# A macaron block on one core: the normed activations 64 bytes short of the weights' address remainder, their 512-column products made as two of 256

## The chip, the cores and the metric

The kernel runs on one core of one Trainium2 chip. The time is the device time of one execution in microseconds (us), as the median of several runs. Before the change it is 1037.92 us, the median of 3 runs from 1037.42 to 1038.10.

## The reference

The input x is one sequence of 512 tokens with 1024 features in float32. One layer is computed, and a final norm:

```python
x = x + 0.5 * swiglu(rms_norm(x, ffn1_norm), ffn1_w_gate, ffn1_w_up, ffn1_w_down)    # 1024 -> 2816 -> 1024
h = rms_norm(x, mix_norm)
z, xbc, dt_raw, u = split(h @ w_in)                     # 1024, 1536, 16 and 1024 columns
y_ssd = ssd_group(z, xbc, dt_raw, ...)                  # conv, scan over chunks, gate, grouped norm
y_pool = multiscale_pool_group(u, pool_w, pool_scale)   # trailing means, a map for each group
x = x + concat([y_ssd, y_pool]) @ w_out
x = x + 0.5 * swiglu(rms_norm(x, ffn2_norm), ffn2_w_gate, ffn2_w_up, ffn2_w_down)
return rms_norm(x, final_norm)
# swiglu(h, wg, wu, wd) = (silu(h @ wg) * (h @ wu)) @ wd
```

## The kernel before

Activations lie feature by feature: a tile is 128 features (partitions) by 512 tokens (columns), and x has DK = 8 such tiles in `xT`. All large products are made with float32 operands that are split into a high part (fp32r) and what is left of it: `whi` and `wlo` for weights, `xghi` and `xglo` for the normed input ("normed" is x times the gain; the division by the root mean square comes later, through `rstd`). A product of two such pairs takes three matmuls: whi by hi, whi by lo, wlo by hi. Each matmul has its own weight load of 128 x 128, also where the weights are the same as in the matmul before.

The work is a sequence of units. A unit has one slot of a ring of RING = 4 in `whi` and `wlo`, holding 8 weight blocks of 128 x 128. ScalarE rounds a fetched weight into `whi` (lines 644, 653, 657), VectorE subtracts to get `wlo` (lines 967, 972), and TensorE waits for both through the semaphores `w_hi` and `w_lo`. A unit of 512 columns has 24 matmuls of 512 columns. Each engine's order is written out by hand.

Each of the two feed-forward stages (FFN1, FFN2) first computes some gate and up units directly: `direct`, by way of `products` (lines 1525 to 1540), 512 columns from `xghi` and `xglo`. FFN1 has 8 such units, of which the first four are computed in pieces by `part` at the start of the kernel (lines 1675 to 1692, matmuls on 1684, 1687, 1690), and FFN2 has 4. The rest of gate and up is made in "quads": two tiles of gate and up together, as a 2 x 2 block product (blocks of features by token halves) with seven products where eight would be the plain way (Strassen's scheme, Winograd's form). FFN1 has 9 quads and FFN2 has 10. A quad is seven units A11, SUM1, SUM2, A12, SUM3, SUM4, A22 by `product` (matmuls on lines 1601 to 1603), each of 24 matmuls of 256 columns. A11, A12 and SUM4 stream halves of `xghi` and `xglo`; SUM1, SUM2, SUM3 and A22 stream `thi` and `tlo`, combinations of the normed input that are made once in each stage. After the quads of a group come eight down units (lines 1619 to 1621), 512 columns from `acthi` and `actlo`; there are three groups in a stage. VectorE gathers the results of the quads (line 1062), forms the sums of weights (lines 1033 to 1055) and the activations, and GpSimd scales gates by `rstd` (line 547).

Between the two stages lies the mixer. `dt_unit` (lines 1785 to 1797) makes a short product of 512 columns from `xghi` and `xglo`. Then 12 + 16 units go through `project` (the convolved channels, z and u), with small products for the scan between them, then the pooled maps, then 8 units of the output projection of the pooled half, and 8 units of that of the other half, from `mixhi` and `mixlo`. In the first two of these groups and in the 8 pooled units the moving operand is `xghi` and `xglo` by 512 columns (lines 1537 to 1539).

Buffers are placed by hand in part. `sb(...)` puts tensors one behind the other: `whi`, `wlo`, `xT`, `xghi`, `xglo`, `rstd`, `sq`, `sumsq`, `ones`, and so on, down to small ones. The tensors placed by `at(...)` have given offsets from `base`. The remainder of an address by 256 bytes is named in constants: WEIGHT_LANE = 128 and HALF_LANE = 192, with LANES = 256.

```python
base += (WEIGHT_LANE - base) % LANES
acthi = at("acthi", 16 * KB, [P, UB * S], F32R)
thi = at("thi", 64 * KB + HALF_LANE, [P, 4, KH, HALF], F32R)
tlo = at("tlo", 80 * KB + HALF_LANE, [P, 4, KH, HALF], F32R)
```

So `whi`, `wlo`, `xghi`, `xglo`, `acthi`, `actlo`, `mixhi`, `mixlo` start at remainder 128. `thi` and `tlo` start at (128 + 192) mod 256 = 64, and `post` and `gbuf` too. All blocks within these tensors are multiples of 512 bytes long, so the remainder is the same for each block of them.

Of the kernel before, what the change touches and what calls it, by code (L numbers as in the profile page):

```python
# [23 lines left out]
P = 128  # L24
S = 512
D = 1024
DK = D // P
# [4 lines left out]
HEADS = 16  # L32
# [3 lines left out]
LOW = 32  # L36
# [4 lines left out]
HALF = S // 2  # L41
# [8 lines left out]
UB = 8  # L50
LANES = 256
WEIGHT_LANE = 128
HALF_LANE = 192
# [68 lines left out]
U_OUTP = U_POOL + 2  # L122
U_OUTS = U_OUTP + DK
M_FFN2 = M_MIX + U_OUTS + DK
# [71 lines left out]
U_ORDER = (6, 7, 4, 5, 2, 3, 0, 1)  # L196
# [3 lines left out]
def cols(tile):  # L200

    return slice(tile * S, (tile + 1) * S) if isinstance(tile, int) else bass.ds(tile * S, S)
# [10 lines left out]
def build(nc, t, out):  # L213
    with ExitStack() as ctx:
        def sb(name, shape, dt=F32):
            return ctx.enter_context(nc.sbuf_tensor(name, shape, dt))
# [5 lines left out]
        whi = sb("w_hi_part", [P, RING, UB, P], F32R)  # L222
        wlo = sb("w_lo_part", [P, RING, UB, P], F32R)
        xT = sb("xT", [P, DK * S])
        xghi = sb("xghi", [P, DK * S], F32R)
        xglo = sb("xglo", [P, DK * S], F32R)
        rstd = sb("rstd", [P, S])
# [6 lines left out]
        eps = sb("eps", [P, 1])  # L234
        inv_count = sb("inv_count", [P, PAD])
        dt_bias = sb("dt_bias", [2 * LOW, 1])
        fold = sb("fold", [2 * LOW, HEADS])
        a_exp = sb("a_exp", [P, HEADS])
        skip_row = sb("skip_row", [P, HEADS])
        skip_col = sb("skip_col", [P, DK])  # L240
        tok_rms = sb("tok_rms", [P, 2, NC])
        neg_gain = sb("neg_gain", [P, 2, DK])
# [70 lines left out]
        PB = [ctx.enter_context(nc.psum_tensor(f"bank{i}", [P, S], F32)) for i in range(8)]  # L313
# [66 lines left out]
        def slot(m):  # L380
            return m % RING
# [25 lines left out]
        def half(h):  # L407
            return slice(h * HALF, (h + 1) * HALF)
# [1112 lines left out]

        @blk.tensor
        def _(pe):
            def products(bank, m, i, blocks, hi, lo, k0, first=True, last=True, ready=None,
                         order=None, midway=None):

                pe.wait_ge(w_hi, i * RING + (m + 1))
                pe.wait_ge(w_lo, i * RING + (m + 1))
                s = slot(m)
                for n, k in enumerate(order or range(blocks)):  # L1530
                    if midway and n == blocks // 2:
                        midway()
                    if ready:
                        pe.wait_ge(ready[0], ready[1] + n + 1)
                    h, l = hi[:, cols(k0 + k)], lo[:, cols(k0 + k)]
                    w, wl = whi[:, s, k, :], wlo[:, s, k, :]
                    pe.matmul(bank, w, h, start=first and n == 0, stop=False)  # L1537
                    pe.matmul(bank, w, l, start=False, stop=False)  # L1538
                    mm = pe.matmul(bank, wl, h, start=False, stop=last and n == blocks - 1)  # L1539
                mm.then_inc(unit_done, 1)  # L1540
# [6 lines left out]
            def direct(f, it, n):  # L1547

                tile, bank = it.tile, it.raw % 4
                if f == 0:  # L1550
                    pe.wait_ge((g_scaled, act_ready)[it.part], tile - 1)
                products(PB[bank][:, :], n, 0, UB, xghi, xglo, 0, ready=(xg_lo, 2 * DK) if n == M_FFN2 else None)

            def moving(f, part, k):

# [121 lines left out]
            def part(m, *ks):  # L1677

                bank = PB[m][:, :]
                h = ks[0] // (UB // 2)  # L1680
                pe.wait_ge((first_hi, w_hi)[h], m + 1)
                for k in ks:
                    pe.wait_ge(xg_hi, k + 1)
                    pe.matmul(bank, whi[:, m, k, :], xghi[:, cols(k)], start=k == 0, stop=False)
                for k in ks:
                    pe.wait_ge(xg_lo, k + 1)
                    pe.matmul(bank, whi[:, m, k, :], xglo[:, cols(k)], start=False, stop=False)
                pe.wait_ge((first_lo, w_lo)[h], m + 1)
                for k in ks:
                    mm = pe.matmul(bank, wlo[:, m, k, :], xghi[:, cols(k)], start=False, stop=k == DK - 1)  # L1690
                if ks[-1] == DK - 1:
                    mm.then_inc(unit_done, 1)

# [30 lines left out]
            M = M_MIX  # L1724
# [6 lines left out]
            def project(m, ready=None, midway=None):  # L1731
                if m >= 2:
                    pe.wait_ge(proj_read, m - 1)
                products(PB[m % 2][:, :], M + m, 0, UB, xghi, xglo, 0, ready=ready, midway=midway)

            def chunks_to_tokens(bank, src, width=P, off=0, rows=P):
                for c in range(NC):
# [136 lines left out]
            for d in range(DK):  # L1874
                if d >= 2:
                    pe.wait_ge(proj_read, U_POOL + d - 1)
                products(PB[(U_OUTP + d) % 2][:, :], M + U_OUTP + d, 0, UB, xghi, xglo, 0,
                         ready=(pool_lo, 0) if d == 0 else None, order=U_ORDER if d == 0 else None)
                if d == 3:
                    for g in range(GROUPS):  # L1880
                        pe.wait_ge(ysum_own, 2 + 4 * (g + 1))
                        pe.matmul(scratch(SC[f"stat{g}"])[:, :], ones[:, :], cbuf[:, g, :],
                                  start=True, stop=True).then_inc(scr_ready, 1)
# [72 lines left out]
```

## Time and profile before

| | |
|---|---|
| median of 3 runs | 1037.92 us |
| the profiled execution | 1038.42 us |
| its span (first to last instruction) | 1036.6 us |
| TensorE matmul busy | 999.3 us (96%), 6118 matmuls |
| TensorE weight loads busy | 878.2 us (85%), 6118 loads |
| VectorE busy | 781.8 us (75%) |
| ScalarE, GpSimd busy | 462.3 us (45%), 212.0 us (20%) |
| mean granted TensorE clock | 0.983 of full |

Durations of matmuls overlap: a matmul of 512 columns is shown with some 0.39 us and one of 256 with 0.28 us, but the next one starts before it ends. So the pace of TensorE is read from the starts of matmuls or of whole units, and not from the mean durations. All times in the views are from the start of the span.

### The profile page before, as it was taken

To read this page: it belongs to the slowest core of one execution; us is meant where nothing else is said; L and a number is where in the kernel's file an instruction comes from. 1 tells how busy PE (TensorE), PEld (TensorE's weight loads), DVE (VectorE), ACT (ScalarE), POOL (GpSimd) and SP (SyncE) were. 2 spreads that over 40 slices of the span, in tenths; PEclk is the share of its full clock that TensorE was granted. 3 is DMA by queue.
4 is the path that set the end of the run, shared out by engine and by line. 5 is a ranking of instruction groups with operands and counts; after the bars stand their busy time and mean duration, and the time that the engine had idled before them with its cause. 6 is when DMAs were issued, how large, how long until landed. Compare 5 with 4: busy or idle time off the path is not lost. (4 is left out here: it accounts for less than half of the span.)

```text
span 1036.6 us, 15358 instructions
## 1 busy us (share of the span) xinstructions
PE 999.3 (96%) x6118; PEld 878.2 (85%) x6118; DVE 781.8 (75%) x983; ACT 462.3 (45%) x603; POOL 212.0 (20%) x179
## 2 busy tenths in 40 slices
PE   9979999999999989999999999879999999999996
PEld 7879889998999658878787888759988999889975
DVE  5788568985697778787699796677966798567864
ACT  6455225552354446653234653344632455325532
POOL 1003002320031242321063452101110113001321
PEclk9989999999999989999999999979999999999998
DMA  8405313442232242322322233422252225412402
GB/s 270 138 24 158 104 41 110 136 143 82 61 103 62 64 125 84 94 65 78 82 82 68 75 89 95 122 82 82 83 162 82 82 82 153 134 41 85 119 21 82
DMA packets 188655, 99.63 MB, mean 96 GB/s; under 512 B 3524, under 2 KB 187944, under 8 KB 188584
## 3 DMA queue, kind: packets, MB, share of 16 engines
q1 hardware_dynamic: 187912, 97.60, 32.2%
q8 instruction: 49, 0.80, 0.3%
q10 hardware_dynamic: 672, 1.05, 0.3%
q14 instruction: 22, 0.18, 0.1%
HBM read 96.54 MB, written 2.10 MB: 95 GB/s over the span
## 5 line engine op out<-in xcount | busy, mean ns | idle before, releaser
L547 POOL TENSOR_TENSOR post<-post,rstd 128x256 f32<-128x256 f32 x57 | 93.3, 1637 | 536.5 <-DVE post L1062 536.5
L1601 PE MATMUL bank<-thi,w_hi_part 128*128 128x256 f32 x608 | 169.5, 279 | 5.8 <-DVE tlo L1023 3.6
L1602 PE MATMUL bank<-tlo,w_hi_part 128*128 128x256 f32 x608 | 168.9, 278 | 0.0
L1603 PE MATMUL bank<-thi,w_lo_part 128*128 128x256 f32 x608 | 168.7, 277 | 0.0
L1537 PE MATMUL bank<-xghi,w_hi_part 128*128 128x512 f32 x352 | 143.5, 408 | 10.4 <-DVE xglo L977 10.4
L972 DVE TENSOR_TENSOR w_lo_part<-w_raw,w_hi_part 128x1024 fp32r<-128x1024 f32 (+1 forms) x102 | 124.8, 1224 | 22.0 <-ACT w_hi_part L644 12.3
L1619 PE MATMUL bank<-acthi,w_hi_part 128*128 128x512 f32 x346 | 136.2, 394 | 4.4 <-DVE upd L1103 2.4
L1538 PE MATMUL bank<-xglo,w_hi_part 128*128 128x512 f32 x352 | 138.5, 393 | 0.0
L1539 PE MATMUL bank<-xghi,w_lo_part 128*128 128x512 f32 x352 | 138.4, 393 | 0.0
L1621 PE MATMUL bank<-acthi,w_lo_part 128*128 128x512 f32 x346 | 134.8, 390 | 0.0
L1620 PE MATMUL bank<-actlo,w_hi_part 128*128 128x512 f32 x346 | 134.7, 389 | 0.0
L1603 PE MATMUL bank<-xghi,w_lo_part 128*128 128x256 f32 x456 | 128.8, 282 | 0.0
L1601 PE MATMUL bank<-xghi,w_hi_part 128*128 128x256 f32 x456 | 128.7, 282 | 0.0
L1602 PE MATMUL bank<-xglo,w_hi_part 128*128 128x256 f32 x456 | 128.4, 282 | 0.0
L1601 PEld LDWEIGHTS bank<-thi,w_hi_part 128*128 128x128 f32 x608 | 115.0, 189 | 6.4 <-DVE tlo L1023 3.8
L1602 PEld LDWEIGHTS bank<-tlo,w_hi_part 128*128 128x128 f32 x608 | 115.1, 189 | 0.0
L1603 PEld LDWEIGHTS bank<-thi,w_lo_part 128*128 128x128 f32 x608 | 114.9, 189 | 0.0
L653 ACT ACTIVATE w_hi_part<-w_raw 128x1024 fp32r<-128x1024 f32 x76 | 80.3, 1056 | 73.9 <-PE bank L1603 38.9
L967 DVE TENSOR_TENSOR w_lo_part<-w_raw,w_hi_part 128x1024 fp32r<-128x1024 f32 x76 | 106.0, 1401 | 0.0
L657 ACT ACTIVATE w_hi_part<-w_raw 128x1024 fp32r<-128x1024 f32 (+1 forms) x56 | 55.9, 998 | 112.3 <-PE bank L1621 74.0
L1103 DVE SCALAR_TENSOR_TENSOR upd<-bank,rstd 128x512 f32<-128x512 f32 (+1 forms) x49 | 33.2, 677 | 91.6 <-PE bank L1621 91.1
L653 ACT ACTIVATE w_hi_part<-wsum 128x1024 fp32r<-128x1024 f32 x57 | 60.3, 1058 | 76.6 <-PE bank L1603 41.6
(260 smaller groups left out, 1958.1 us busy)
## 6 DMA issues: line engine op xcount, KB each, us to landing
w_raw<-in_ffn_w_gate SPq DMA_DIRECT2D x42, 512.0 KB, 3.7
w_raw<-in_ffn_w_up SPq DMA_DIRECT2D x42, 512.0 KB, 4.6
w_raw<-in_ffn_w_down SPq DMA_DIRECT2D x32, 512.0 KB, 4.4
w_raw<-in_w_in SPq DMA_DIRECT2D x29, 512.0 KB, 3.6
w_raw<-in_w_out SPq DMA_DIRECT2D x16, 512.0 KB, 3.9
w_raw<-in_ffn_w_down SPq DMA_DIRECT2D x16, 384.0 KB, 4.1
out<-xtok SPq DMA_DIRECT2D x4, 512.0 KB, 3.1
xload<-in_x SPq DMA_DIRECT2D x3, 512.0 KB, 6.7
```

What stands on the lines that cost most here:

```text
L653: act.activation(split(whi, n), weight(q, it.part), ACT.Copy).then_inc(w_hi, 1)
L967: dve.tensor_tensor(split(wlo, n), weight(it.quad, it.part), split(whi, n).bitcast(F32), ALU.subtract).then_inc(w_lo, 1)
L972: dve.tensor_tensor(wlo[:, slot(n), 0:blocks], raw[:, src, 0:blocks], whi[:, slot(n), 0:blocks].bitcast(F32), ALU.subtract).then_inc(w_lo, 1)
L1537: pe.matmul(bank, w, h, start=first and n == 0, stop=False)
L1538: pe.matmul(bank, w, l, start=False, stop=False)
L1539: mm = pe.matmul(bank, wl, h, start=False, stop=last and n == blocks - 1)
L1601: pe.matmul(out, w, hi, start=opens and e == 0 and k == 0, stop=False, skip_group_check=True)
L1602: pe.matmul(out, w, lo, start=False, stop=False, skip_group_check=True)
L1603: mm = pe.matmul(out, wl, hi, start=False, stop=end, skip_group_check=True)
L1619: pe.matmul(bank, whi[:, s, k, :], h, start=first and k == ks[0], stop=False)
L1620: pe.matmul(bank, whi[:, s, k, :], l, start=False, stop=False)
L1621: mm = pe.matmul(bank, wlo[:, s, k, :], h, start=False, stop=last and k == ks[-1])
```

## The change

The small tensors `fold`, `a_exp` and `skip_row` (64 bytes in each partition, 192 in all) move from behind `dt_bias` to a place ahead of `xghi`. By this `xghi`, `xglo`, `rstd`, `sq`, `sumsq`, `ones`, `ident`, `causal`, `par`, `eps`, `inv_count` and `dt_bias` lie 192 bytes further, at remainder 64 for those that were at 128. `skip_col` and all that follows stays where it was. Every product whose moving operand is `xghi` or `xglo` by 512 columns (in `part`, `direct`, `project` and the pooled half of the output projection) is made as two matmuls of 256 columns, into the two halves of the same bank: the first half of the columns and then the second, with the same weights, before the next of the three products. The short product in `dt_unit` keeps its 512 columns. The products of the quads, of down and from `mixhi` keep their form.

```diff
--- before.py
+++ after.py
@@ -222,6 +222,10 @@
         whi = sb("w_hi_part", [P, RING, UB, P], F32R)
         wlo = sb("w_lo_part", [P, RING, UB, P], F32R)
         xT = sb("xT", [P, DK * S])
+        fold = sb("fold", [2 * LOW, HEADS])
+        a_exp = sb("a_exp", [P, HEADS])
+        skip_row = sb("skip_row", [P, HEADS])
+        assert nc.sbuf_base % LANES == (WEIGHT_LANE + HALF_LANE) % LANES
         xghi = sb("xghi", [P, DK * S], F32R)
         xglo = sb("xglo", [P, DK * S], F32R)
         rstd = sb("rstd", [P, S])
@@ -234,9 +238,6 @@
         eps = sb("eps", [P, 1])
         inv_count = sb("inv_count", [P, PAD])
         dt_bias = sb("dt_bias", [2 * LOW, 1])
-        fold = sb("fold", [2 * LOW, HEADS])
-        a_exp = sb("a_exp", [P, HEADS])
-        skip_row = sb("skip_row", [P, HEADS])
         skip_col = sb("skip_col", [P, DK])
         tok_rms = sb("tok_rms", [P, 2, NC])
         neg_gain = sb("neg_gain", [P, 2, DK])
@@ -1521,6 +1522,27 @@
 
         @blk.tensor
         def _(pe):
+            def both_halves(bank, w, x, k, start=False, stop=False):
+                for h in range(2):
+                    mm = pe.matmul(bank[:, half(h)], w, x[:, k * S + h * HALF:k * S + (h + 1) * HALF],
+                                   start=start and h == 0, stop=stop, skip_group_check=True)
+                return mm
+
+            def from_norm(bank, m, ready=None, order=None, midway=None):
+
+                pe.wait_ge(w_hi, m + 1)
+                pe.wait_ge(w_lo, m + 1)
+                s = slot(m)
+                for n, k in enumerate(order or range(UB)):
+                    if midway and n == UB // 2:
+                        midway()
+                    if ready:
+                        pe.wait_ge(ready[0], ready[1] + n + 1)
+                    both_halves(bank, whi[:, s, k, :], xghi, k, start=n == 0)
+                    both_halves(bank, whi[:, s, k, :], xglo, k)
+                    mm = both_halves(bank, wlo[:, s, k, :], xghi, k, stop=n == UB - 1)
+                mm.then_inc(unit_done, 1)
+
             def products(bank, m, i, blocks, hi, lo, k0, first=True, last=True, ready=None,
                          order=None, midway=None):
 
@@ -1549,7 +1571,7 @@
                 tile, bank = it.tile, it.raw % 4
                 if f == 0:
                     pe.wait_ge((g_scaled, act_ready)[it.part], tile - 1)
-                products(PB[bank][:, :], n, 0, UB, xghi, xglo, 0, ready=(xg_lo, 2 * DK) if n == M_FFN2 else None)
+                from_norm(PB[bank][:, :], n, ready=(xg_lo, 2 * DK) if n == M_FFN2 else None)
 
             def moving(f, part, k):
 
@@ -1681,13 +1703,13 @@
                 pe.wait_ge((first_hi, w_hi)[h], m + 1)
                 for k in ks:
                     pe.wait_ge(xg_hi, k + 1)
-                    pe.matmul(bank, whi[:, m, k, :], xghi[:, cols(k)], start=k == 0, stop=False)
+                    both_halves(bank, whi[:, m, k, :], xghi, k, start=k == 0)
                 for k in ks:
                     pe.wait_ge(xg_lo, k + 1)
-                    pe.matmul(bank, whi[:, m, k, :], xglo[:, cols(k)], start=False, stop=False)
+                    both_halves(bank, whi[:, m, k, :], xglo, k)
                 pe.wait_ge((first_lo, w_lo)[h], m + 1)
                 for k in ks:
-                    mm = pe.matmul(bank, wlo[:, m, k, :], xghi[:, cols(k)], start=False, stop=k == DK - 1)
+                    mm = both_halves(bank, wlo[:, m, k, :], xghi, k, stop=k == DK - 1)
                 if ks[-1] == DK - 1:
                     mm.then_inc(unit_done, 1)
 
@@ -1731,7 +1753,7 @@
             def project(m, ready=None, midway=None):
                 if m >= 2:
                     pe.wait_ge(proj_read, m - 1)
-                products(PB[m % 2][:, :], M + m, 0, UB, xghi, xglo, 0, ready=ready, midway=midway)
+                from_norm(PB[m % 2][:, :], M + m, ready=ready, midway=midway)
 
             def chunks_to_tokens(bank, src, width=P, off=0, rows=P):
                 for c in range(NC):
@@ -1874,8 +1896,8 @@
             for d in range(DK):
                 if d >= 2:
                     pe.wait_ge(proj_read, U_POOL + d - 1)
-                products(PB[(U_OUTP + d) % 2][:, :], M + U_OUTP + d, 0, UB, xghi, xglo, 0,
-                         ready=(pool_lo, 0) if d == 0 else None, order=U_ORDER if d == 0 else None)
+                from_norm(PB[(U_OUTP + d) % 2][:, :], M + U_OUTP + d,
+                          ready=(pool_lo, 0) if d == 0 else None, order=U_ORDER if d == 0 else None)
                 if d == 3:
                     for g in range(GROUPS):
                         pe.wait_ge(ysum_own, 2 + 4 * (g + 1))
```

## Rows read from the trace of the kernel before

**Rows 1.** The page's first part: busy time of each engine.

```profile
PE 999.3 (96%) x6118; PEld 878.2 (85%) x6118; DVE 781.8 (75%) x983; ACT 462.3 (45%) x603; POOL 212.0 (20%) x179
```

**Rows 2.** TensorE groups by line and shape: busy us, mean ns, idle before, releasers.

```profile
L1601 PE MATMUL bank<-thi,w_hi_part 128*128 128x256 f32 x608 | 169.5, 279 | 5.8 <-DVE tlo L1023 3.6 <-DVE w_lo_part L967 1.9 <-ACT post L701 0.3
...
L1537 PE MATMUL bank<-xghi,w_hi_part 128*128 128x512 f32 x352 | 143.5, 408 | 10.4 <-DVE xglo L977 10.4
...
L1619 PE MATMUL bank<-acthi,w_hi_part 128*128 128x512 f32 x346 | 136.2, 394 | 4.4 <-DVE upd L1103 2.4 <-DVE actlo L1000 1.6
...
L1601 PE MATMUL bank<-xghi,w_hi_part 128*128 128x256 f32 x456 | 128.7, 282 | 0.0
```

**Rows 3.** TensorE's timeline: first matmuls of A11, SUM1, SUM2, A12.

```profile
187.16 0.28 PE L1601 MATMUL bank<-xghi,w_hi_part 128*128 128x256 f32 x1
...
190.02 0.29 PE L1601 MATMUL bank<-thi,w_hi_part 128*128 128x256 f32 x1
...
192.76 0.28 PE L1601 MATMUL bank<-thi,w_hi_part 128*128 128x256 f32 x1
...
195.48 0.28 PE L1601 MATMUL bank<-xghi,w_hi_part 128*128 128x256 f32 x1
```

**Rows 4.** Timeline of TensorE: first matmuls of two direct units, 24 matmuls apart.

```profile
40.40 0.39 PE L1537 MATMUL bank<-xghi,w_hi_part 128*128 128x512 f32 x1
...
45.84 0.39 PE L1537 MATMUL bank<-xghi,w_hi_part 128*128 128x512 f32 x1
```

**Rows 5.** TensorE's timeline: halves of the last down unit, matmuls 1 and 9.

```profile
1019.68 0.28 PE L1925 MATMUL bank<-acthi,w_hi_part 128*128 128x256 f32 x1
...
1020.63 0.28 PE L1927 MATMUL bank<-acthi,w_lo_part 128*128 128x256 f32 x1
```

**Rows 6.** One quad's window: us, PE, PEld, DVE, ACT, POOL, clock, DMA, GB/s.

```profile
187.16:206.68 19.52, 19.52 (x171) 19.52 (x169) 18.83 (x21) 11.03 (x14) 4.98 (x4) 1.00 0.39 115
```

**Rows 7.** Timeline of VectorE in that quad.

```profile
196.30 1.21 DVE L967 TENSOR_TENSOR w_lo_part<-wsum,w_hi_part 128x1024 fp32r<-128x1024 f32 x1
...
198.54 0.69 DVE L1062 TENSOR_TENSOR post<-post,bank 128x512 f32<-128x512 f32 x1 [0.69 <-PE bank L1603]
...
200.28 1.76 DVE L967 TENSOR_TENSOR w_lo_part<-w_raw,w_hi_part 128x1024 fp32r<-128x1024 f32 x1
```

**Rows 8.** Timeline of TensorE in the first quad: two stalls.

```profile
61.65 0.35 PE L1601 MATMUL bank<-thi,w_hi_part 128*128 128x256 f32 x1 [1.90 <-DVE w_lo_part L967]
...
66.50 0.58 PE L1601 MATMUL bank<-thi,w_hi_part 128*128 128x256 f32 x1 [3.56 <-DVE tlo L1023]
```

**Rows 9.** The chain of waits ahead of FFN2's first down unit.

```profile
760.33 1.15 DVE actlo L1000
761.62 0.47 PE bank L1619
```

**Rows 10.** TensorE's timeline: restarts behind small products, 512 and 256 columns.

```profile
390.75 0.50 PE L1537 MATMUL bank<-xghi,w_hi_part 128*128 128x512 f32 x1
391.09 0.39 PE L1538 MATMUL bank<-xglo,w_hi_part 128*128 128x512 f32 x1
...
1022.36 0.36 PE L1925 MATMUL bank<-acthi,w_hi_part 128*128 128x256 f32 x1
1022.56 0.28 PE L1926 MATMUL bank<-actlo,w_hi_part 128*128 128x256 f32 x1
```

**Rows 11.** Timeline of TensorE: the short product's last stall.

```profile
374.69 0.63 PE L1794 MATMUL bank<-xglo,w_hi_part 128*32 128x512 f32 x1 [4.51 <-DVE xglo L977]
```

**Rows 12.** Groups by line and shape: ScalarE, sources and targets at different remainders.

```profile
L653 ACT ACTIVATE w_hi_part<-w_raw 128x1024 fp32r<-128x1024 f32 x76 | 80.3, 1056 | 73.9 <-PE bank L1603 38.9 <-PE bank L1621 35.0
...
L693 ACT ACTIVATE thi<-t 128x1024 fp32r<-128x1024 f32 x8 | 8.5, 1060 | 19.2 <-DVE t L1011 19.2
```

**Rows 13.** Windows at the lower clock (columns as in rows 6).

```profile
674.00:687.70 13.70, 6.17 (x13) 4.18 (x14) 8.40 (x11) 7.31 (x9) 1.26 (x1) 0.50 0.38 112
373.60:380.50 6.90, 5.81 (x12) 3.79 (x13) 5.59 (x4) 3.53 (x4) 6.61 (x6) 0.51 0.52 149
```

## The prediction

> **What bounds the kernel now.** I began with the busy times on the page: TensorE matmuls 999.3 of 1036.6 us, no other engine over 76% [rows 1]. The groups by line say whether the rest can matter: with all the idle time ahead of them, the product lines wait 5.8 us for thi, 10.4 us for the 512-column products from xghi, 4.4 us in down, and nothing for the 256-column products from xghi [rows 2]. So the end is set by the pace at which TensorE streams matmuls, stage after stage. That pace is not the mean duration (matmuls overlap in the rows, and by their means two of 256 columns would look dearer, 2 x 279 ns, than one of 512 with 408 ns [rows 2]), so I read starts on the timeline.
>
> In a quad all units have 24 matmuls of 256 columns, the same shape and the same number of weight loads. From the start of A11 to that of SUM1 there are 190.02 - 187.16 = 2.86 us, SUM1 takes 2.74 us, SUM2 2.72 us [rows 3]. The pattern repeats to 10 ns in all steady quads: a unit that streams xghi and xglo takes 2.86 us (119.2 ns a matmul), one that streams thi and tlo takes 2.74 us directly behind an xghi unit and 2.72 us otherwise (113.3 ns). What differs in the code is the address remainder of the moving operand: 128 as the weights, or 64. The last down unit checks this: it streams acthi, remainder 128, by 256 columns, from a quite different place in memory, and its eight intervals take 0.95 us, 118.8 ns each [rows 5]. So 119 ns goes with the weights' own remainder, 113.3 with the other.
>
> A unit of 24 matmuls of 512 columns at remainder 128 takes 45.84 - 40.40 = 5.44 us [rows 4], 226.7 ns a matmul. That is twice 113.3.
>
> **The change part by part.**
>
> *256-column units from xghi (A11, A12, SUM4).* They come to remainder 64 with no other edit. There are 57 of them, three in each of 19 quads. I price them as SUM2: 2.86 - 2.72 = 0.14 us less. SUM1, SUM3 and A22 no longer follow a slower unit: 2.74 - 2.72 = 0.02 us less each. A steady quad goes from 19.52 us [rows 6] to 7 x 2.72 = 19.04 us, 0.48 us less. The cost of an xghi unit at the new place is not in the trace; below it is bounded by a loss of nothing seen (2.86 us stays), above by 2.72, and I take 2.72, the row with the same shape, engine and remainder.
>
> Quads with the full gain: 18 x 0.48 = 8.64 us. The first quad of FFN1 is different: SUM1 waits for w_lo until 61.65 and then for tlo until 66.50 [rows 8], VectorE's work, so A11's gain there goes into the stall. A12 to A22 keep 2 x 0.14 + 2 x 0.02 = 0.32 us. At the end of the six groups the chain runs from the gather after SUM4 through VectorE to actlo, which ends last, 761.62 [rows 9]; what A22 saves there is waited for instead: 6 x 0.02 = 0.12 us back. Sum: 8.64 + 0.32 - 0.12 = 8.84 us.
>
> *Does VectorE keep up?* In a middle quad it is busy 18.83 of 19.52 us, idle 0.69 [rows 6], and that idle time is a wait for TensorE's bank [rows 7]. Two quads, the middle ones of FFN1's second group and of FFN2's second group, are that tight; the others are idle 1.2 us or more. A gain of 0.48 us leaves 0.21 us idle, so VectorE stays just behind TensorE and not ahead of it. The cover is thin: one w_lo subtraction in that quad took 1.76 us [rows 7]. I take no loss; the other end is below, as a rival.
>
> *512-column products as two of 256.* 48 units: the 4 of `part`, 4 direct in FFN1, 4 direct in FFN2, 28 of `project`, 8 of the pooled output projection, so 48 x 24 = 1152 matmuls become 2304, with 1152 more weight loads. In steady flow 2 x 113.3 = 226.6 ns against 226.7 ns: nothing. More weight loads cost nothing at that pace, since the thi units keep one load per 256 columns at 113.3 ns. Alternating between the halves of a bank, where the quads write one half for 12 matmuls, is not shown; the 512-column matmul writes both in turn, and I take it as free. The ends for this edit: at 119.2 ns a half, 2 x 119.2 - 226.7 = 11.7 ns more for each of 1152, 13.5 us slower; below, as far under the thi rows as the xghi rows are over them, 107.4 ns a half, 13.7 us faster (an estimate of mine for the end only); the thi rows have shape and remainder in common with what is made, and I keep them.
>
> *Restarts.* Behind small products the first interval of a unit is 0.34 us for 512 columns against 0.227 in flow, 0.11 more; for 256 columns 0.20 against 0.12, 0.08 more [rows 10]. About 20 units of the mixer start so: 20 x 0.03 = 0.6 us less. I take 0.5, with ends at 0 and 1.2 (the following intervals are some ns slow as well by 512 columns).
>
> *The short product* keeps 512 columns at remainder 64, which no row shows. It waits for xglo in any case, 4.51 us at its last block [rows 11]; two matmuls follow, so even twice their time is under 0.5 us. I take 0.
>
> *Engines that read or write the moved tensors.* ScalarE's copy of 1024 columns takes 1056 ns from w_raw into whi and 1060 ns from t32 into thi, at other remainders on both sides [rows 12]. So a new remainder costs ScalarE nothing here; I take the same for VectorE and GpSimd. No wait, DMA or queue order changes.
>
> *The sum.* 8.84 + 0.5 = 9.3 us less. From the profiled 1038.42 us (span 1036.6) that is 1029.1 us. That execution lies 0.5 us above the median shown, so the forecast is 1037.9 - 9.3 = **1028.6 us**.
>
> *Two rules weighed.* The equality 226.7 = 2 x 113.3 is from rows 3 and 4. The Trainium skill, "TensorE: Matmul & The Clock Gate", section "Back-to-back issue gap", gives a warm gap of the columns by 2.4 GHz plus 2.5 ns for each matmul; by that, 1152 more matmuls would cost 2.9 us, and the sum would be 6.4 us less instead of 9.3. The trace disagrees with its figures (215.8 and 109.2 ns against 226.7 and 113.3). That page also has a sustained roofline of 131 ns for 512 columns with their loads, which the trace contradicts (226.7 ns).
>
> **The rivals.**
>
> *A: halves cost as the other halves at 119 ns (slower).* If the remainder is not what parts the two kinds of unit, but something that thi has and xghi has not, xghi stays at 119.2 ns after the move. Then the quads gain nothing and the split costs 1152 x 11.7 ns = 13.5 us, less 0.5 for restarts: 1051 us. The price falls in `part`, the direct units, `project` and the pooled projection, and decides from the first product on; the whole change turns slower as soon as a matmul of 256 columns from xghi takes over 115.8 ns, 2.5 above 113.3 (9.3 us over the 57 x 24 in the quads and the 2304 halves). For it: no row shows xghi at 64. Against it: acthi, which is neither in xghi's place nor in thi's, goes with its remainder [rows 5]. The Trainium skill, "SBUF — State Buffer", section "Who interferes with whom", gives TensorE two independent read ports, for moving operand and weight load, and says that it never waits on anyone; by that rule a remainder could change nothing and this rival would hold. Rows 3 speak against the rule.
>
> *B: VectorE becomes the bound in the quads.* If collisions with GpSimd stretch its work (1.76 us against 1.21 us for the same shape [rows 7]), TensorE would wait for w_lo, and half of the quads' gain would turn into idle time ahead of line 1601: 8.84 / 2 + 0.5 = 4.9 us less, 1033 us. For it: 0.21 us of cover. Against: only two quads are so tight.
>
> *C: the clock's low stretches move.* TensorE ran at the lower level, 1.2 GHz, from 674.0 to 687.7 us with 6.17 us of matmuls and from 373.6 to 380.5 with 5.81 us [rows 13], each behind a stall. Work at half speed loses half of its time, 3.1 and 2.9 us. Stages now begin 4 and 9 us earlier, and the switch back may come earlier or later against the work: one stretch longer by half gives 1.5 us more, 1030.2 us, and shorter ones up to 3 us less, 1025.6 us. Small shifts of this kind belong to the forecast's own range.
>
> **How the numbers follow.** Forecast 0.74, with its own range of 1027 to 1030.5 us; A 0.08; B 0.08; C, off by over 1.5 us, 0.10. The range reaches from 1025.5 (C below, restarts at their end) to 1034 (B); A stays outside. A measurement of this kernel tells about 0.2%, 2.1 us, from no change. Faster by more: forecast, C and most of B, 0.89. Within: 0.03. Slower: 0.08, A.
>
> **What would show it.** The starts of A11 and SUM1 2.72 us apart and a steady quad of 19.04 us; direct and `project` units still 5.44 us, now with 48 matmuls; some 7270 matmuls in all, and weight loads close to 100% busy in the mixer; VectorE idle some 0.2 us in the tight quads with no wait for w_lo ahead of TensorE there; the stall before 66.50 us unchanged at its end. Units of 2.86 us in the quads and 5.72 us in `project` would make it wrong (A), and waits of line 1601 for w_lo in each quad would show B.

## The result, and the profile after

The change makes the kernel slower: median 1040.47 us (1039.08 to 1045.20, 14 runs) against 1037.91 us (1036.39 to 1038.72, 14 runs). The ratio is 1.0034, 95% interval 1.0022 to 1.0046, some 3.5 us (the medians alone are 2.6 us apart). The forecast was 1028.6 us, the range 1025.5 to 1034. The profiled execution took 1044.33 us with a span of 1042.6 us, 3.9 us above the median of its kernel; why is among the findings. Times are more spread than before, 6.1 us from lowest to highest against 2.3 us.

The page's first part and four groups of TensorE by line and shape answer to [rows 1, 2]. Line 1527 is the helper `both_halves`.

```profile
PE 1006.6 (97%) x7270; PEld 934.7 (90%) x7270; DVE 781.8 (75%) x983; ACT 461.4 (44%) x603; POOL 212.0 (20%) x179
```

```profile
L1623 PE MATMUL bank<-thi,w_hi_part 128*128 128x256 f32 x608 | 171.8, 283 | 5.9 <-DVE tlo L1024 3.6 <-DVE w_lo_part L968 2.1 <-ACT post L702 0.3
...
L1527 PE MATMUL bank<-xghi,w_hi_part 128*128 128x256 f32 x768 | 154.8, 287 | 10.7 <-DVE xglo L978 10.3 <-ACT xghi L662 0.3
...
L1641 PE MATMUL bank<-acthi,w_hi_part 128*128 128x512 f32 x346 | 136.3, 394 | 3.9 <-DVE upd L1104 2.3 <-DVE actlo L1001 1.4
...
L1623 PE MATMUL bank<-xghi,w_hi_part 128*128 128x256 f32 x456 | 127.9, 280 | 0.0
```

There are 7270 matmuls, as computed, and the waits are the old ones to 0.5 us. But the mean of the thi products rose from 279 to 283 ns, though neither `thi` nor its products were touched. That line is the first sign: the loss is in TensorE's pace and not in a wait. The timeline of TensorE, first matmuls of units, shows two paces. First an xghi unit and the thi unit behind it, in the first group of FFN1, then A11, SUM1, SUM2 and A12 of quad 4 (compare [rows 3]), then two units of the pooled output projection, then two more (compare [rows 4]):

```profile
79.77 0.28 PE L1623 MATMUL bank<-xghi,w_hi_part 128*128 128x256 f32 x1
...
82.49 0.28 PE L1623 MATMUL bank<-thi,w_hi_part 128*128 128x256 f32 x1
...
85.21 0.28 PE L1623 MATMUL bank<-xghi,w_hi_part 128*128 128x256 f32 x1
...
188.01 0.28 PE L1623 MATMUL bank<-xghi,w_hi_part 128*128 128x256 f32 x1
...
190.84 0.28 PE L1623 MATMUL bank<-thi,w_hi_part 128*128 128x256 f32 x1
...
193.67 0.28 PE L1623 MATMUL bank<-thi,w_hi_part 128*128 128x256 f32 x1
...
196.50 0.28 PE L1623 MATMUL bank<-xghi,w_hi_part 128*128 128x256 f32 x1
...
580.30 0.28 PE L1527 MATMUL bank<-xghi,w_hi_part 128*128 128x256 f32 x1
...
585.95 0.28 PE L1527 MATMUL bank<-xghi,w_hi_part 128*128 128x256 f32 x1
...
610.09 0.28 PE L1527 MATMUL bank<-xghi,w_hi_part 128*128 128x256 f32 x1
...
615.53 0.28 PE L1527 MATMUL bank<-xghi,w_hi_part 128*128 128x256 f32 x1
```

Near 80 us a unit takes 2.72 us, 113.3 ns a matmul, as forecast. Near 190 us each unit takes 2.83 us, 117.8 ns, whether it streams xghi or thi. The same is seen for 48 matmuls: 5.65 us at 580 and 5.44 us at 610, from the same buffers by the same line. In the quads, a pace holds from the start of an unbroken stretch of 256-column matmuls to its end; in the mixer some units take up to five intervals to settle. Group 1 of FFN1 ran at the fast one; groups 2 and 3 of FFN1 and all of FFN2's quads at the slow one, 17 of 19 quads. In the mixer 16 of 36 units ran at the slow one. A slow steady quad takes 19.79 us, where it was 19.52 us [rows 6] and 19.04 us was forecast.

Where the 6.0 us between the two profiled spans came from, by the starts of the same units on the two timelines:

| place | before | after | added since the row above |
|---|---|---|---|
| first unit after `part` | 34.95 | 35.81 | +0.85 |
| quad 2 (FFN1's second group) | 148.11 | 148.44 | -0.52 |
| short product | 365.94 | 367.96 | +1.69 |
| quad 9 (FFN2's first) | 702.47 | 706.11 | +1.62 |
| last group of down in FFN2 | 986.46 | 992.45 | +2.35 |

The two rows that hold nothing but slow quads and down units, +1.69 and +2.35, are 4.0 of the 6.0 us.

### The profile page after: what moved, and what is told of

Same layout as the page of the kernel before. It is cut to its first block and busy times, and to the rows that moved or that the text cites. A ratio compares the mean times of both kernels' runs of the same rounds, so it can differ in the third digit from the quotient of the medians.

```text
span 1042.6 us, 17662 instructions
## 1 busy us (share of the span) xinstructions
PE 1006.6 (97%) x7270; PEld 934.7 (90%) x7270; DVE 781.8 (75%) x983; ACT 461.4 (44%) x603; POOL 212.0 (20%) x179
## 5 line engine op out<-in xcount | busy, mean ns | idle before, releaser
L1623 PE MATMUL bank<-thi,w_hi_part 128*128 128x256 f32 x608 | 171.8, 283 | 5.9 <-DVE tlo L1024 3.6
L1624 PE MATMUL bank<-tlo,w_hi_part 128*128 128x256 f32 x608 | 171.3, 282 | 0.0
L1625 PE MATMUL bank<-thi,w_lo_part 128*128 128x256 f32 x608 | 171.2, 282 | 0.0
L1527 PE MATMUL bank<-xghi,w_hi_part 128*128 128x256 f32 x768 | 154.8, 287 | 10.7 <-DVE xglo L978 10.3
L1527 PE MATMUL bank<-xghi,w_lo_part 128*128 128x256 f32 x768 | 148.8, 280 | 0.7 <-DVE w_lo_part L1182 0.6
L1527 PE MATMUL bank<-xglo,w_hi_part 128*128 128x256 f32 x768 | 149.4, 280 | 0.1
L1527 PEld LDWEIGHTS bank<-xghi,w_hi_part 128*128 128x128 f32 x768 | 117.5, 190 | 17.6 <-DVE xglo L978 10.7
L1623 PE MATMUL bank<-xghi,w_hi_part 128*128 128x256 f32 x456 | 127.9, 280 | 0.0
L1624 PE MATMUL bank<-xglo,w_hi_part 128*128 128x256 f32 x456 | 127.9, 280 | 0.0
L1625 PE MATMUL bank<-xghi,w_lo_part 128*128 128x256 f32 x456 | 127.9, 280 | 0.0
L1625 PEld LDWEIGHTS bank<-thi,w_lo_part 128*128 128x128 f32 x608 | 117.3, 193 | 0.0
L1527 PEld LDWEIGHTS bank<-xghi,w_lo_part 128*128 128x128 f32 x768 | 116.0, 189 | 1.1 <-DVE w_lo_part L1182 1.1
L1527 PEld LDWEIGHTS bank<-xglo,w_hi_part 128*128 128x128 f32 x768 | 116.6, 190 | 0.3 <-DVE xglo L978 0.3
```

The costliest lines, as they stand in the source:

```text
L1527: mm = pe.matmul(bank[:, half(h)], w, x[:, k * S + h * HALF:k * S + (h + 1) * HALF], start=start and h == 0, stop=stop, skip_group_check=True)
L1623: pe.matmul(out, w, hi, start=opens and e == 0 and k == 0, stop=False, skip_group_check=True)
L1624: pe.matmul(out, w, lo, start=False, stop=False, skip_group_check=True)
L1625: mm = pe.matmul(out, wl, hi, start=False, stop=end, skip_group_check=True)
```

## The experiments

Ratios are against runs of the kernel before on the same chip. Theory P says: a stream of 256-column matmuls, each with its weight load, has more than one steady pace, and which one it holds is set when it is entered.

**Split alone.** `fold`, `a_exp` and `skip_row` go back behind `dt_bias`.

```diff
-        fold = sb("fold", [2 * LOW, HEADS])
-        a_exp = sb("a_exp", [P, HEADS])
-        skip_row = sb("skip_row", [P, HEADS])
...
         xghi = sb("xghi", [P, DK * S], F32R)
...
         dt_bias = sb("dt_bias", [2 * LOW, 1])
+        fold = sb("fold", [2 * LOW, HEADS])
+        a_exp = sb("a_exp", [P, HEADS])
+        skip_row = sb("skip_row", [P, HEADS])
```

> The 512-column products from xghi are made as two of 256, and nothing is moved (xghi stays at remainder 128). Theory P (two paces: a stream of 256-column matmuls with its weight loads runs at 113.3 or at 117.8 ns a matmul at remainder 64, whichever it falls into when it is entered, and at 119 to 120 ns at remainder 128): each of the 48 split units takes 48 x 119.8 = 5.75 us instead of 5.44 us, some 13 us slower in all, 1050 to 1051 us, and the quads stay at 19.52 us with thi at 113.3 ns. Rival S (the split itself is free, and what slows the changed kernel is the place of the moved tensors): about 1037 us. Rival H (the doubled number of instructions slows TensorE's queue): some 4 us slower, without a change of pace in steady flow.

Measured: 1048.70 us, ratio 1.0105 (1.0088 to 1.0122), 10.8 us slower. Its timeline, two direct units, 5.76 us apart:

```profile
42.09 0.28 PE L1526 MATMUL bank<-xghi,w_hi_part 128*128 128x256 f32 x1
...
47.85 0.28 PE L1526 MATMUL bank<-xghi,w_hi_part 128*128 128x256 f32 x1
```

That is 120 ns a matmul at remainder 128, in all of the split units, and the quads stayed at 19.52 us. So the remainder does matter, as the prediction had it. The steady price is 0.32 us a unit, 15 us for all 48, of which the median shows 10.8. Part of the rest is seen on the timeline: the stall of FFN1's first quad took up 1.4 us (that quad starts 2.66 us late and takes 1.37 us less), restarts are shorter by halves, and FFN2's first direct unit took 6.71 us where it was 7.69, behind 3.60 us of matmuls at the lower clock where [rows 13] have 6.17.

**Move alone.** All products keep their form, the small tensors stay ahead of `xghi`.

Against the kernel before, the move is all of the edit:

```diff
         xT = sb("xT", [P, DK * S])
+        fold = sb("fold", [2 * LOW, HEADS])
+        a_exp = sb("a_exp", [P, HEADS])
+        skip_row = sb("skip_row", [P, HEADS])
...
         xghi = sb("xghi", [P, DK * S], F32R)
```

> xghi, xglo and their neighbours are moved to remainder 64, and all products keep their 512 columns. Theory P: the quads are one stream at remainder 64 that is entered behind 512-column down units without a gap, so 117.8 ns a matmul and 19.79 us a quad in five of the six groups, 4 to 5 us slower in the quads; the direct and projecting units show what 512 columns cost at remainder 64, which nothing has shown yet (226.7 ns if the remainder doesn't matter there): 1041 us or more. Rival H (the split is what costs): the quads run at 113.3 ns, 19.04 us each, and the time is near 1029 us. Rival S: as theory P in sign, but thi and xghi units of a quad at different paces.

Measured: 1043.81 us, ratio 1.0061 (1.0045 to 1.0078). The timeline: two direct units of 512 columns, then A11 of quads 4, 5, 9 and 10.

```profile
40.94 0.40 PE L1538 MATMUL bank<-xghi,w_hi_part 128*128 128x512 f32 x1
...
46.54 0.40 PE L1538 MATMUL bank<-xghi,w_hi_part 128*128 128x512 f32 x1
...
188.41 0.28 PE L1602 MATMUL bank<-xghi,w_hi_part 128*128 128x256 f32 x1
...
208.19 0.28 PE L1602 MATMUL bank<-xghi,w_hi_part 128*128 128x256 f32 x1
...
707.17 0.28 PE L1602 MATMUL bank<-xghi,w_hi_part 128*128 128x256 f32 x1
...
726.22 0.28 PE L1602 MATMUL bank<-xghi,w_hi_part 128*128 128x256 f32 x1
```

The 512-column products cost 5.60 us a unit, 233.3 ns each, at remainder 64, against 5.44 us [rows 4]; those from `mixhi`, which did not move, stayed at 226.7 ns in the same run. So the split was needed for them: even slow halves (5.65 us) lose hardly more, and fast halves (5.44 us) nothing. Quads are slow (19.79 us) in five groups with no split anywhere, so it isn't the split that slows them. Only FFN2's first group is fast (19.04 us).

**The changed kernel again.**

> The changed kernel once more, for a second profile. Theory P: the stretches right behind 512-column units (the quads of the second and third groups of FFN1 and of the groups in FFN2) run at 117.8 ns again, and those behind a wait or small products (the units of the mixer, the first group of FFN1) run at 113.3 or 117.8 in another pattern than in the first profile, which makes the spread of its times (1039 to 1045 us). Rival S or H: the same pace in the same stretches, and the spread is not in TensorE's pace.

Measured: 1040.60 us (1040.13 to 1044.03), ratio 1.0030 (1.0018 to 1.0043). Its timeline has quad 9 fast, 19.04 us, where the first profile had 19.79 us:

```profile
704.79 0.28 PE L1623 MATMUL bank<-xghi,w_hi_part 128*128 128x256 f32 x1
...
723.83 0.28 PE L1623 MATMUL bank<-xghi,w_hi_part 128*128 128x256 f32 x1
```

The same program thus had another pace in the same stretch (FFN2's direct units with quads 9 to 11): that stretch starts behind the stall for xglo. The groups behind down units were slow again. FFN1's first group, also entered from a stall, was slow this time and fast in the first profile. The mixer's units had the same pace in both. The first profile is 4.3 us longer. The stretch in FFN2 makes 3.2 us of it, 2.7 by the pace and 0.5 by more matmuls at the lower clock in its first unit; FFN1's first group makes 0.9 us the other way. The first unit behind the short product (7.72 against 6.83 us, from matmuls at the lower clock) adds 0.9, and the last matmuls of the kernel, 213 against 112 ns each, 0.8. So the spread of the times has two parts, as far as two profiles show: the pace in stretches that start behind a stall, and where the lower clock ends or begins.

**Extra matmuls of several sizes.** One matmul with a discarded result, ahead of A11 in 15 quads.

```diff
+KICK = {3: 8, 4: 16, 5: 32, 6: 64, 7: 96, 8: 128, 10: 192, 11: 224, 12: 48, 13: 24, 14: 80, 15: 112, 16: 160, 17: 2, 18: 64}
...
+                if part == A11 and q in KICK:
+                    pe.matmul(PB[7][:, 0:KICK[q]], whi[:, slot(n), 0, :], xghi[:, 0:KICK[q]], start=True, stop=True)
```

> The changed kernel with one extra small matmul ahead of A11 in 15 of the 19 quads, into a bank that nobody reads: 8, 16, 32, 64, 96, 128 columns in quads 3 to 8, and 192, 224, 48, 24, 80, 112, 160, 2, 64 in quads 10 to 18. Theory P: the pace changes at some of these places, between 113.3 and 117.8 ns, and holds until the next one or the end of the stretch; quads at 113.3 take 19.04 us. Rival S or H: the pace stays as it was and the extra matmul costs its own time of some 0.1 us.

Measured: one run, 1037.02 us. The timeline at quads 3, 4 and 5, behind 8, 16 and 32 extra columns, then quad 6 and quad 18, each with its 64 extra columns and the starts of A11 and SUM1:

```profile
167.43 0.36 PE L1626 MATMUL bank<-xghi,w_hi_part 128*128 128x256 f32 x1
...
187.30 0.17 PE L1617 MATMUL bank<-xghi,w_hi_part 128*128 128x16 f32 x1
187.33 0.36 PE L1626 MATMUL bank<-xghi,w_hi_part 128*128 128x256 f32 x1
...
206.47 0.18 PE L1617 MATMUL bank<-xghi,w_hi_part 128*128 128x32 f32 x1
206.50 0.36 PE L1626 MATMUL bank<-xghi,w_hi_part 128*128 128x256 f32 x1
...
270.46 0.19 PE L1617 MATMUL bank<-xghi,w_hi_part 128*128 128x64 f32 x1
270.49 0.36 PE L1626 MATMUL bank<-xghi,w_hi_part 128*128 128x256 f32 x1
...
273.32 0.28 PE L1626 MATMUL bank<-thi,w_hi_part 128*128 128x256 f32 x1
...
965.69 0.19 PE L1617 MATMUL bank<-xghi,w_hi_part 128*128 128x64 f32 x1
965.72 0.36 PE L1626 MATMUL bank<-xghi,w_hi_part 128*128 128x256 f32 x1
...
968.63 0.28 PE L1626 MATMUL bank<-thi,w_hi_part 128*128 128x256 f32 x1
```

Quad 3 stays slow (19.87 us with its extra matmul), quad 4 turns fast (19.14), quad 5 slow again. Over all 15: behind 16, 64 (quad 6), 128, 192, 224, 24, 112 and 2 columns the quad ran fast, behind 8, 32, 96, 48, 80, 160 and 64 (quad 18) slow. The same 64 columns thus led to 2.83 us for A11 and a fast quad at one place and to 2.91 us and a slow quad at the other, so the size alone doesn't decide. What differs is the stream before: quad 6 follows down units, quad 18 a fast quad. Of the 12 extra matmuls put between two quads nine turned the pace over (16, 128, 24, 112 and 2 columns from slow to fast; 32, 96, 80 and 64 from fast to slow), and three left it (8 slow; 192 and 224 fast). Behind down units 64 led to fast, 48 and 160 to slow. An otherwise idle matmul of some 0.1 us can switch the next stretch in either direction. Theory P holds; the rivals that blame the split or the place don't.

**64 extra columns at 14 entries, and 48 as a control.** Into the unit's own bank, whose first product clears it.

```diff
+KICK = 64
...
+                if part == A11 and (not QUADS[q].chained) and q:
+                    pe.matmul(bank[:, 0:KICK], whi[:, slot(n), 0, :], xghi[:, 0:KICK], start=True, stop=True)
...
-                project(U_Z + h)
+                project(U_Z + h, kick=KICK if h % 2 else 0)
...
+                          kick=KICK if d == 0 else 0)
```

> The changed kernel with one extra matmul of 64 columns (from xghi, with the first weights of the unit, into the unit's own bank before its first product) in front of 14 streams that are entered behind 512 columns: A11 of the first quad of five groups (quads 2, 6, 9, 12, 16), the eight odd z and u units, and the first unit of the pooled output projection. Theory P (two paces, chosen at the entry): with this size each stretch of quads falls into 113.3 ns a matmul, as quads 6 and 18 did behind 64 columns, so 17 quads take 19.04 us and not 19.79 us, 12.8 us less than with all of them slow; the extra matmuls cost 0.12 us each, 1.7 us; 12 units of the mixer at 5.44 us give back up to 2.5 us. Together 1029 to 1033 us, faster than before. Rival (the pace is chosen anew at random at each entry, or the 64 columns were luck): some of the five stretches stay at 117.8 ns, and the time is between 1036 and 1042 us with a wide spread.

> As the kernel with 64 extra columns, but with 48. Theory P with the phase of the stream as what decides: 48 columns put quad 12 at 117.8 ns, so the stretches of quads stay slow behind this size, and the time is 1040 to 1046 us. Rival (any extra matmul breaks the pattern): as with 64 columns, 1029 to 1033 us.

Measured with 64: 1033.95 us (1032.90 to 1035.23), ratio 0.9964 (0.9951 to 0.9978). With 48: one run, 1046.58 us. Both lie up to 1 us above the ranges expected. The first timeline is of 64 columns, A11 of quads 3 and 4, then of 9 and 10; the second of 48, quads 3 and 4.

```profile
167.33 0.28 PE L1628 MATMUL bank<-xghi,w_hi_part 128*128 128x256 f32 x1
...
186.37 0.28 PE L1628 MATMUL bank<-xghi,w_hi_part 128*128 128x256 f32 x1
...
700.81 0.36 PE L1628 MATMUL bank<-xghi,w_hi_part 128*128 128x256 f32 x1
...
720.68 0.28 PE L1628 MATMUL bank<-xghi,w_hi_part 128*128 128x256 f32 x1
```

```profile
168.79 0.28 PE L1628 MATMUL bank<-xghi,w_hi_part 128*128 128x256 f32 x1
...
188.58 0.28 PE L1628 MATMUL bank<-xghi,w_hi_part 128*128 128x256 f32 x1
```

With 64 columns all four groups entered behind 512-column down units are fast (19.04 us a quad), with 48 all four are slow (19.79 us). The expectation that all five kicked stretches of quads would be fast missed one: quad 9 follows FFN2's direct units, which ran fast here, and the extra matmul threw it into the slow pace (19.87 us). That expectation also took it that quads 6 and 18 had both run fast behind 64 columns; quad 18, entered like quad 9 from a fast stream, had not. In the mixer the eight extra matmuls gained nothing either: seven of the eight units behind them ran at the slow pace. The one at the pooled output projection made its first four units fast and left the last four, fast in the changed kernel, slow.

**Other remainders.** HALF_LANE = 128 and 64, with as many small tensors moved as it takes.

Moving operands are then at remainder 0 and 192, the weights at 128 as before.

```diff
-HALF_LANE = 192
+HALF_LANE = 128
```

```diff
-HALF_LANE = 192
+HALF_LANE = 64
```

> The changed kernel with HALF_LANE = 128 instead of 192: xghi, xglo, thi and tlo (and the tensors behind them) at remainder 0 while the weights stay at 128. It asks whether the second pace is tied to the distance of 64 bytes short. Theory P leaves open which pace another distance has; if it is a matter of when loads and streams of the same 256 bytes meet, the steady pace is another one here (between 113.3 and 120 ns) and the same in all stretches, or there are two again in other stretches. Rival (only 'not the same remainder' matters): the same two paces in the same stretches as at 64, about 1040 us.

> The changed kernel with HALF_LANE = 64: moving operands at remainder 192, 64 bytes past the weights' 128. As for remainder 0: another set of paces if the order in which the two reads come to the same place matters (64 past is not the mirror of 64 short), or the same two paces, about 1040 us, if only the difference matters.

Measured: 1058.22 us, ratio 1.0192 (1.0177 to 1.0208), at remainder 0; 1048.40 us, ratio 1.0100 (1.0085 to 1.0116), at 192. A11 of quads 4 and 5, first at remainder 0, 20.16 us, 120.0 ns a matmul, then at 192, 19.79 us:

```profile
190.70 0.28 PE L1623 MATMUL bank<-xghi,w_hi_part 128*128 128x256 f32 x1
...
210.86 0.28 PE L1623 MATMUL bank<-xghi,w_hi_part 128*128 128x256 f32 x1
```

```profile
189.27 0.28 PE L1623 MATMUL bank<-xghi,w_hi_part 128*128 128x256 f32 x1
...
209.06 0.28 PE L1623 MATMUL bank<-xghi,w_hi_part 128*128 128x256 f32 x1
```

Remainder 0 has two paces as well: 120.0 ns in the quads behind down units and in FFN2, 118.7 ns in FFN1's first group, where a unit takes 2.85 us, and in most units of the mixer. At 192 all quads are slow, FFN1's first group and FFN2's too, and 32 of the mixer's 36 units. It has the narrowest spread (1048.28 to 1048.54). Of the four remainders tried (128 is the split alone), only 64 has the fast pace in whole groups, and it is the best. The weights stayed at remainder 128 in all of them, so it isn't shown whether the moving operand's own remainder counts or its distance from that of the weights.

**64 extra columns at five entries.** Against the kernel with 14 of them, without quad 9 and without the mixer's eight units.

```diff
-                if part == A11 and (not QUADS[q].chained) and q:
+                if part == A11 and q in (2, 6, 12, 16):
...
-                project(U_Z + h, kick=KICK if h % 2 else 0)
+                project(U_Z + h)
```

> The changed kernel with the extra matmul of 64 columns in five places only: A11 of quads 2, 6, 12 and 16, whose stretches begin behind the 512-column down units and ran at 113.3 ns with it, and the first unit of the pooled output projection. Left out are quad 9, which the extra matmul threw from the fast into the slow pace, and the eight units of the mixer, which it did not make faster. Theory P: 9 x 0.12 = 1.1 us less than with 14 extra matmuls, and the first group of FFN2 is left to its entry: 1030.5 to 1033.5 us, at least 4 us faster than before, with a spread of some 2 us by that group. Rival (the stretches fall into a pace at random in each program): some of the four stretches run at 117.8 ns and the time is 1035 us or more.

Measured: 1031.52 us (1030.14 to 1033.70), ratio 0.9937 (0.9924 to 0.9951). It is faster than before by 6.4 us and than the changed kernel by some 9. All 19 quads run at the fast pace here. The gain comes from the four entries of quads: at the pooled output projection three units turned fast and five slow, where the changed kernel had four of each. Its window of quad 4:

```profile
186.72:205.75 19.03, 19.03 (x170) 19.03 (x169) 18.80 (x21) 11.20 (x14) 4.95 (x4) 1.00 0.38 113
```

**The kernel before, with extra matmuls ahead of SUM1.** Nothing moved, nothing split.

```diff
+KICK = {1: 8, 2: 16, 3: 32, 4: 64, 5: 96, 6: 128, 7: 48, 8: 24, 9: 80, 10: 112, 11: 160, 12: 2, 13: 192, 14: 224, 15: 40, 16: 56, 17: 72, 18: 88}
...
+                if part == SUM1 and q in KICK:
+                    pe.matmul(bank[:, 0:KICK[q]], whi[:, slot(n), 0, :], thi[:, 0, 0, 0:KICK[q]], start=True, stop=True)
```

> The kernel before, nothing moved and nothing split, with one extra matmul (from thi) of another number of columns in front of SUM1 in quads 1 to 18, where the moving operand changes from xghi at remainder 128 to thi at remainder 64. Theory P (113.3 ns of the thi units was not a property of their remainder alone, but of how they were entered, behind units at 120 ns): in some of the quads SUM1 and SUM2 run at 117.8 ns, 5.65 us for the two instead of 5.46, while SUM3 and A22, entered as before, stay at 113.3. Rival (the slow pace belongs to the moved layout): SUM1 and SUM2 stay at 113.3 ns in all quads and the extra matmuls cost 0.1 us each, 1040 us.

Measured: one run, 1043.27 us. Quad 4 on its timeline, the extra matmul, then the start of SUM1:

```profile
191.73 0.20 PE L1595 MATMUL bank<-thi,w_hi_part 128*128 128x64 f32 x1
191.76 0.36 PE L1604 MATMUL bank<-thi,w_hi_part 128*128 128x256 f32 x1
```

A12 starts at 197.50 us, so SUM1 and SUM2 take 5.74 us, with 117.8 ns a matmul in steady flow. In 16 of the 18 quads the two fell to 117.8 ns; behind 128 and 112 columns they stayed at 113.3. SUM3 and A22, entered as before, held 114.2 ns (the three slow first intervals included) in every quad. The slow pace was open to thi all along.

## Why the prediction was wrong, step by step

- **The step that failed** is in the first part: "119 ns goes with the weights' own remainder, 113.3 with the other", and with it the price of an xghi unit "as SUM2". The remainder matters, but it doesn't fix the pace: at 64 there are two, 113.3 and 117.8 ns. In the kernel before, each thi unit was entered behind an xghi unit at 120 ns, or from another thi unit, and that entry always led to 113.3. The change put both kinds at one remainder, so a whole group became a single stretch with one entry, and behind a 512-column down unit without an extra matmul that entry led to 117.8 each time. The row that was priced bore the mark of its neighbours. The quads were forecast 8.84 us faster: 17 of 19 in the profile cost 0.27 us more each where steady, not 0.48 less. All 19 together took 3.6 us more, 12.4 us off the forecast, of the 15.3 us between 9.3 us less and the 6.0 us more of the profiled span.
- *Split products, taken as free.* Free at the fast pace (5.44 us), 0.21 us more a unit at the slow one. The bounds held 119.2 ns, but as another theory's price, not as a pace within this one.
- *Restarts.* Right: 0.20 to 0.22 us for the first interval by halves, 398.66 to 398.86 on the timeline.
- *VectorE keeps up.* Right, as far as it was tested: with fast quads it is busy 18.80 of 19.03 us, idle 0.23 where 0.21 was computed, and TensorE is busy throughout that window. Rival B is out for this pace.
- *Rival A.* Its two halves came apart. Its price for 119 ns halves is near what the split alone cost (10.8 of 13 us). Its ground, that the remainder isn't what parts the units, is refuted. None of the rivals had the changed kernel's case, a pace between the two.
- *Rival C.* The lower clock did shift, but in the kernel's favour. Ahead of FFN2's direct units 4.10 us of matmuls fall into it in the first profile and 3.03 in the second, where it was 6.17 [rows 13]. At half speed that is 1.0 and 1.6 us less, so the clock there explains none of the loss and hides some of it; the stretch at the short product holds 5.74 us in the first profile, where it was 5.81 [rows 13]. The windows, first profile, then second:

```profile
679.30:689.70 10.40, 4.10 (x13) 3.07 (x14) 6.34 (x9) 4.62 (x7) 1.27 (x1) 0.51 0.37 108
...
678.10:688.40 10.30, 3.03 (x9) 2.12 (x9) 5.96 (x8) 4.52 (x7) 1.26 (x1) 0.50 0.49 143
```

- *The short product and the other engines.* No row shows a cost: the short product starts and ends 2.02 and 2.03 us late, and VectorE's busy time is 781.8 us in both.
- *The two rules.* The Trainium skill, "SBUF — State Buffer", section "Who interferes with whom", says that TensorE never waits on another engine and reads its two operands through independent ports. What the prediction drew from it, that a remainder could change nothing, is refuted: by a move of buffers alone 512-column matmuls went from 226.7 to 233.3 ns. Whether the two ports disturb each other is not shown, as the weights were never moved. The Trainium skill, "TensorE: Matmul & The Clock Gate", section "Back-to-back issue gap", has one isolated gap for each number of columns; here 256 columns have four in steady flow, 113.3, 117.8, 118.7 and 120.0 ns.

What stays open: why an entry leads to one pace or the other. The weight loads give a clue, but not an answer. In slow quad 4 of the changed kernel the loads of `wlo` take 192 ns and those of `whi` 188; in the fast second quad both take 188. At remainder 192, with the same 117.8 ns a matmul, they take 188 too (the three lines below, in this order). Whether two reads meet in step is thus open. Nor is it shown why 64 columns lead to the fast pace behind down units and to the slow one from a fast stream and in most of the mixer.

```profile
L1625 PEld LDWEIGHTS bank<-thi,w_lo_part 128*128 128x128 f32 x32 | 6.1, 192 | 0.0
...
L1625 PEld LDWEIGHTS bank<-thi,w_lo_part 128*128 128x128 f32 x31 | 5.8, 188 | 0.0
...
L1625 PEld LDWEIGHTS bank<-thi,w_lo_part 128*128 128x128 f32 x32 | 6.0, 188 | 0.0
```

## What to carry to other kernels

A steady pace that is read from a trace belongs to the stream it was measured in, its entry included. Before pricing other work at that pace, look at what comes ahead of each stretch that has it, and ask whether the change keeps that. Where each matmul has its own weight load, read the pace in each stretch from starts, not as one mean. A small extra matmul at an entry (some 0.1 us here) was worth 2.7 us over a group of four quads, but it has to be tried at each entry: the same one cost 2.2 us over three quads where the stream was fast already.

## What the runs showed of the hardware

- With the weights at remainder 128 and a load for each, 256-column matmuls of fp32r ran in steady flow at 113.3 or 117.8 ns with the moving operand at remainder 64, at 117.8 (seldom 113.3) at 192, at 118.7 or 120.0 at 0, and at 120.0 at 128. At 512 columns it is 226.7 ns at 128 and 233.3 ns at 64.
- The pace is a state of the stream. It lasted through up to 80 us of matmuls and through changes of buffer and bank. One small matmul turned it over in 9 of 12 trials between two quads, with as few as 2 columns.
- The same program took either pace in a stretch that starts behind a stall, worth 2.7 us in FFN2.
